# Recurrent mixer: where the convolution's taps stand in VectorE's order around the state scan

## The chip, the cores and the metric

The kernel runs on one core of one Trainium2 chip. The metric is the device time of one execution in microseconds (us). An engine here is TensorE (matrix products), VectorE and ScalarE (elementwise work), GpSimd or the queue that issues transfers. Each executes its own list of instructions in program order and waits on semaphores where the program says so.

## What is computed

Two stacks of transformer blocks over 512 tokens of width 1024, in 32 bits. The change concerns one of their twelve phases, the mixer of the first layer (`mixa` in the kernel). It is half recurrence, half convolution:

```python
def rwkv7_scan(r, w, k, v, kk, a):          # S_t = S_{t-1} diag(w_t) - (S_{t-1} kk_t)(kk_t*a_t)^T + v_t k_t^T
    def step(state, inp):
        r_t, w_t, k_t, v_t, kk_t, a_t = inp
        s_kk = jnp.einsum('bhvk,bhk->bhv', state, kk_t)
        state = (state * w_t[:, :, None, :] - s_kk[..., None] * (kk_t * a_t)[:, :, None, :]
                 + v_t[..., None] * k_t[:, :, None, :])
        return state, jnp.einsum('bhvk,bhk->bhv', state, r_t)
...
    y = rwkv7_scan(rh, hs(decay), kh, vh, kk, hs(a))        # 8 heads of 64
    y = group_norm(y) * lnx_g + lnx_b                       # written out in the reference
    y_a = (y + bonus) * g
    glu = c_val * jax.nn.sigmoid(c_gate)                    # 512 channels
    conv = lax.conv_general_dilated(glu, conv_w[:, None, :], ...) + conv_b   # 31 taps, causal, depthwise
    y_b = jax.nn.silu(layer_norm(conv, conv_ln_g, conv_ln_b, CONV_LN_EPS))
    return jnp.concatenate([y_a, y_b], axis=-1) @ w_out
```

The two halves are independent from the input projection to the concatenation.

## The kernel before

Every phase is a program for each engine: `pe` for TensorE, `act` for ScalarE, `dve` for VectorE, `pool` for GpSimd, `sp` for the queue that loads weights. The order within an engine is written out by hand; a planner has no part in it. Arrays lie with their features on the 128 partitions, in tiles of 128 features by 512 tokens.

The recurrence is computed in 16 chunks of 32 tokens. After the input projection (22 panels), products within the chunks give masked matrices (line 1711, `gram`); VectorE inverts triangular 32x32 matrices for all chunks and heads (lines 2107 and 2108); TensorE turns and multiplies the factors (lines 1718 to 1790) and makes the per-chunk transitions (line 1802, `outer`), which ScalarE copies out of PSUM. Then come token products in rounds (line 1826, `tokens`): after the fourth round VectorE adds their result to `rho` (line 2115), and TensorE goes on with eight more rounds, the first of which needs all four additions.

The scan proper is a loop over chunks c = 1 to 14. In each step TensorE multiplies the transition with the state (line 1844) and signals `fs_done`, and multiplies the state with `rho` for the output (line 1849). VectorE scales the state (line 2121), adds the outer product (line 2122), waits for `fs_done`, and adds the product in two halves to make the next state (line 2128), which signals `state_ready`, for which TensorE's next step waits.

After the scan ScalarE copies the output y (line 1943), TensorE sums it by heads (line 1854), VectorE centres it (line 2131), ScalarE squares it (line 1946), TensorE sums the squares (line 1691), and ScalarE takes four roots (line 1949, `head_roots` up to 5). VectorE makes the reciprocals (line 2134). TensorE spreads them over the partitions (line 1698, `head_spread`), and only behind that in its order come the column sums of the convolution's layer norm (line 1863), for which all 124 taps must be done (`conv_tap`). VectorE centres the convolution's result with them (line 2138), finishes the normed y (lines 2141 to 2143), and so on to the output projection, which begins at line 243.

The convolution is a list of 31 x 4 = 124 taps in VectorE's program. `conv(n)` issues the next n of them: the first four are a scaling with the bias (line 2065), the others multiply a shifted `glu` by a weight and add it to `acc` (line 2068). A tap needs nothing but the tap of four places before it and `glu`, which is complete long before. Nothing but the layer norm reads the result. In the kernel before, 44 taps stand ahead of the additions to `rho`, one in each of the 14 steps of the scan, and the other 66 behind the centring of y, ahead of the reciprocals.

Of the kernel before, what the change touches and what calls it, by code (L numbers as in the profile page):

```python
# [1612 lines left out]
def make_mixa(env):  # L1613
# [33 lines left out]
    def state(c):  # L1647
        return E2[0][:, 0] if c == 1 else S2[0][:, c - 2] if c < 10 else S2[1][:, c - 10]
# [315 lines left out]
    def dve(dve, idx, n, b):  # L1964
# [84 lines left out]
        def masked(kind, banks, dst, m):  # L2049
            for par in range(2):  # L2050
                dve.wait_ge(S("mats_done"), 2 * kind + par + 1)
                tt(dst[:, 16 * par:16 * par + 16, :], PS[:, banks[par], :].rearrange("p (h s) -> p h s", h=16),
                   con(m).unsqueeze(1).to_broadcast([128, 16, C]), ALU.mult).then_inc(S("mats_masked"), 1)

        taps = [(j, f) for j in range(CONVW) for f in range(4)]
        done = [0]

        def conv(count):

            for _ in range(min(count, len(taps) - done[0])):  # L2060
                j, f = taps[done[0]]
                src, w = glu[:, f, j:j + T], vec("cw", 4 * j + f)
                if j == 0:
                    dve.wait_ge(S("glu_made"), 4)
                    i = ve.tensor_scalar(acc[:, f, :], src, w, vec("cb", f), ALU.mult, ALU.add)
                else:
                    dve.wait_ge(S("conv_tap"), done[0] - 3)
                    i = stt(out=acc[:, f, :], in0=src, scalar=w, in1=acc[:, f, :], op0=ALU.mult, op1=ALU.add)  # L2068
                i.then_inc(S("conv_tap"), 1)
                done[0] += 1  # L2070
# [38 lines left out]
        ve.transpose(Tt.rearrange("p h t -> p t h"), Tp).then_inc(S("inverse"), 1)  # L2109
        masked(2, (6, 7), Gt, "mupi")  # L2110
        masked(3, (1, 2), Qt, "mupin")
        conv(44)
        for f in range(4):
            dve.wait_ge(S("round_done"), 4)
            tt(rho[:, f, :], rho[:, f, :], PS[:, BB[f], :], ALU.add).then_inc(S("factors_made"), 1)
        dve.wait_ge(S("ef_copied"), 16)
        for c in range(1, NCH - 1):
            if c > 1:
                dve.wait_ge(S("state_ready"), 2 * (c - 1))
            d = steps[c % 2]  # L2120
            st.done(tt(d, state(c), ends[:, :, c:c + 1].to_broadcast([128, NHP, 64]), ALU.mult))
            st.done(tt(d, d, E2[c // 8][:, c % 8], ALU.add))
            conv(1)
            dve.wait_ge(S("fs_done"), c)
            for par in range(2):
                rows = slice(64 * par, 64 * par + 64)
                f_s = PS[rows, BA[2 * (c % 2) + par], 0:256].rearrange("p (h v) -> p h v", h=NHP)
                tt(state(c + 1)[rows], d[rows], f_s, ALU.add).then_inc(S("state_ready"), 1)
        for f in range(4):
            dve.wait_ge(S("gn_sums"), f + 1)  # L2130
            stt(out=y[:, f, :], in0=PS[:, BA[f], :], scalar=-1.0 / HD, in1=y[:, f, :], op0=ALU.mult, op1=ALU.add).then_inc(S("centred"), 1)
        conv(len(taps))
        dve.wait_ge(S("head_roots"), 5)
        ve.reciprocal(recips, sums).then_inc(S("head_recips"), 1)
        dve.wait_ge(S("conv_tap"), 4 * CONVW)
        dve.wait_ge(S("gn_sums"), 13)
        for f in range(4):
# [11 lines left out]
        env["parts_dve"](dve, b["mix"], DT, HI0)  # L2149

    return dict(sp=sp, pool=pool, pe=pe, act=act, dve=dve, hi0=HI0)


# [125 lines left out]
```

## Time and profile before

| | us |
|---|---|
| three runs | 3999.42, 4002.21, 4023.23 |
| median of them | 4002.21 |
| the profiled execution | 3997.31 |
| its span | 3995.5 |

| engine | busy, us | share of the span |
|---|---|---|
| TensorE, products | 3707.4 | 93% |
| VectorE | 1927.5 | 48% |
| ScalarE | 1505.7 | 38% |
| GpSimd | 13.5 | 0% |

How to read it: the span is from the first to the last instruction of the profiled execution, and 1.8 us lie around it. The shares are averages over twelve phases; the mixer's recurrence takes less than 250 us of the span. The granted clock is TensorE's, as a part of 2.4 GHz: 1.00 is that, 0.50 is 1.2 GHz. The idle time that the timeline shows before an instruction carries the name of the engine and line that released it.

### The profile page before, as it was taken

How to read it: one execution, taken by the hardware profiler on the slowest of the kernel's cores; microseconds unless marked ns; L12 is line 12 of the kernel's file. 1: busy time of each engine (PE TensorE's matmuls, PEld its weight loads, DVE VectorE, ACT ScalarE, POOL GpSimd, SP SyncE). 2: the span in 40 equal slices, each digit the busy share in tenths (PEclk: the TensorE clock that was granted, in tenths of full speed). 3: DMA queues.
4: the chain of work that ended last, by engine and by line, in shares of the span. 5: the costliest groups of instructions: out<-in, count | busy, mean ns of one | idle time of the engine just before them, and what ended most of it. 6: DMA issues, size and time to landing. Idle time of an engine off the chain costs nothing.

```text
span 3995.5 us, 56056 instructions
## 1 busy us (share of the span) xinstructions
PE 3707.4 (93%) x21784; PEld 3056.4 (76%) x21784; DVE 1927.5 (48%) x2830; ACT 1505.7 (38%) x2293; POOL 13.5 (0%) x33
## 2 busy tenths in 40 slices
PE   8999986499999999999999998889999989899998
PEld 6887765378887887996678887668788876687887
DVE  3443476744425443234444424545676344456763
ACT  3323421243323333335443234544444335454432
POOL 0000000000000000000000000000000000000000
PEclk9999986699999999999999999999999989999999
DMA  3323210023232233220022332002232320023333
GB/s 112 99 92 97 69 54 4 6 79 99 94 96 79 97 94 94 90 89 6 19 80 97 93 94 87 1 17 90 85 100 92 96 86 1 27 81 94 96 95 94
DMA packets 84246, 297.16 MB, mean 74 GB/s; under 512 B 9520, under 2 KB 9520, under 8 KB 83696
## 3 DMA queue, kind: packets, MB, share of 16 engines
q1 hardware_dynamic: 82512, 288.24, 23.0%
q0 software_dynamic: 1568, 6.56, 0.5%
q8 instruction: 122, 2.00, 0.2%
q14 instruction: 44, 0.36, 0.0%
HBM read 292.66 MB, written 2.10 MB: 74 GB/s over the span
## 4 chain that ended last, share of the span: by engine, by line
PE 88%; DVE 6%; ACT 3%; issue 2%; DMA 1%; SPq 0%; DVEq 0%; ACTq 0%
PE PS L252 21%; PE PS L243 21%; PE PS L244 20%; PE PS L834 4%; PE PS L857 3%; PE PS L329 2%; PE PS L332 2%; PE PS L330 2%; PE PS L363 2%; PE PS L846 2%; DVE WK L2068 1%; PE PS L922 1%; PE PS L836 1%; PE PS L275 1%; ACT WHI L215 1%
## 5 line engine op out<-in xcount | busy, mean ns | idle before, releaser
L243 PE MATMUL PS<-WK_R,WHI 128*128 128x512 f32 (+1 forms) x3712 | 1443.8, 390 | 14.0 <-ACT WK_R L581 11.0
L244 PE MATMUL PS<-WK_R,WLO 128*128 128x512 f32 (+1 forms) x3712 | 1438.6, 388 | 0.0
L219 DVE TENSOR_TENSOR WLO<-RAW,WHI 128x1024 fp32r<-128x1024 f32 x563 | 689.2, 1225 | 1266.9 <-ACT WHI L215 1263.6
L215 ACT ACTIVATE WHI<-RAW 128x1024 fp32r<-128x1024 f32 x563 | 596.9, 1060 | 1038.8 <-PE PS L252 838.4
L243 PEld LDWEIGHTS PS<-WK_R,WHI 128*128 128x128 f32 x3712 | 699.5, 188 | 168.8 <-issue 20.2
L244 PEld LDWEIGHTS PS<-WK_R,WLO 128*128 128x128 f32 x3712 | 699.4, 188 | 141.7 <-issue 0.7
L252 PE MATMUL PS<-H_LO,WHI 128*128 128x512 f32 x2712 | 683.1, 391 | 4.5 <-DVE H_LO L436 4.2
L252 PEld LDWEIGHTS PS<-H_LO,WHI 128*128 128x128 f32 x2712 | 508.3, 188 | 119.8 <-DVE H_LO L436 16.3
L252 PE MATMUL PS<-HID_LO,WHI 128*128 128x512 f32 x1056 | 263.2, 389 | 0.0
L252 PEld LDWEIGHTS PS<-HID_LO,WHI 128*128 128x128 f32 x1056 | 198.0, 188 | 40.9
L329 PE MATMUL PS<-WHI,WK_R 128*128 128x256 f32 (+1 forms) x736 | 190.4, 291 | 5.0 <-DVE WLO L219 4.9
L330 PE MATMUL PS<-WLO,WK_R 128*128 128x256 f32 (+1 forms) x736 | 189.9, 290 | 0.0
L1004 DVE SCALAR_TENSOR_TENSOR SC<-SC,VEC 128x511 f32<-128x511 f32 x176 | 132.2, 751 | 111.5 <-ACT SC L971 99.6
L834 PE MATMUL PS<-WK 64*128 64x512 f32 (+5 forms) x384 | 178.3, 549 | 5.8 <-ACT WK L1121 3.4
L609 ACT ACTIVATE WK_R<-HID (+1 forms) x88 | 55.7, 633 | 261.0 <-DVE HID L626 261.0
L329 PEld LDWEIGHTS PS<-WHI,WK_R 128*128 128x128 f32 x736 | 140.4, 191 | 5.8 <-DVE WLO L219 3.8
L897 DVE TENSOR_REDUCE AS<-PS 128x1 f32<-128x512 f32 (+2 forms) x192 | 111.1, 580 | 65.3 <-PE PS L834 62.8
L971 ACT ACTIVATE SC<-SC,VEC 128x512 f32<-128x512 f32 x88 | 72.0, 818 | 182.3 <-DVE SC L994 182.3
L330 PEld LDWEIGHTS PS<-WLO,WK_R 128*128 128x128 f32 x736 | 140.5, 191 | 0.0
L606 ACT ACTIVATE SC<-SC 128x512 f32<-128x512 f32 x88 | 55.7, 632 | 159.4 <-DVE SC L620 159.0
L628 DVE TENSOR_TENSOR HID_LO<-HID,WK_R (+1 forms) x88 | 61.0, 693 | 86.8 <-ACT WK_R L609 86.8
L363 PEld LDWEIGHTS PS<-CON,SC 128*128 128x128 f32 x640 | 87.0, 202 | 18.0 <-ACT SC L511 6.7
(325 smaller groups left out, 3538.0 us busy)
## 6 DMA issues: line engine op xcount, KB each, us to landing
RAW<-in_ffn_gu SPq DMA_DIRECT2D x176, 512.0 KB, 3.4
RAW<-in_f_up SPq DMA_DIRECT2D x88, 512.0 KB, 3.7
RAW<-in_ffn_dn SPq DMA_DIRECT2D x64, 512.0 KB, 3.6
RAW<-in_c_in SPq DMA_DIRECT2D x32, 512.0 KB, 3.5
RAW<-in_f_dn SPq DMA_DIRECT2D x32, 512.0 KB, 3.5
RAW<-in_ffn_dn SPq DMA_DIRECT2D x32, 384.0 KB, 3.1
RAW<-in_a_in SPq DMA_DIRECT2D x22, 512.0 KB, 3.4
RAW<-in_b_out SPq DMA_DIRECT2D x16, 512.0 KB, 3.5
```

Source lines behind the costliest of these rows:

```text
L215: nc.scalar.activation(WHI[:, slot, :], RAW[:, slot, :], ACT.Copy).then_inc(S("w_hi"), 1)
L219: nc.vector.tensor_tensor(WLO[:, slot, :], RAW[:, slot, :], WHI[:, slot, :].bitcast(F32), ALU.subtract).then_inc(S("w_lo"), 1)
L243: pe.matmul(o, WHI[:, slot, w], hi(k), start=(first and b_ == 0), stop=False)
L244: pe.matmul(o, WLO[:, slot, w], hi(k), start=False, stop=False)
L252: mm = pe.matmul(o, WHI[:, p.nslot(s_), w], lo(k), start=False, stop=(last and b_ == len(ks) - 1))
L329: pe.matmul(o, hi(k, t), WHI[:, slot, w], start=(first and b_ == 0), stop=False)
L330: pe.matmul(o, hi(k, t), WLO[:, slot, w], start=False, stop=False)
L363: mm = pe.matmul(PS[:, b_, 128 * t:128 * t + 128], SC[:, k, 128 * t:128 * t + 128], ones, start=(first and t == 0), stop=(last and t == TT ...
L834: mm = pe.matmul(o, spec["q"](h, t), spec["k"](h, n), start=True, stop=extra is None)
L857: mm = pe.matmul(PS[:, 5 + U % 2, 0:spec["dv"]], spec["PT"](U % 3)[:, 128 * b:128 * b + 128], v, start=(b == 0), stop=(b == nb - 1))
L897: nc.vector.reduce_max(stat(1, U), PS[:, U % 3, 0:n], AX.X, negate=True).then_inc(S("at_max"), 1)
L1004: nc.vector.scalar_tensor_tensor(out=o, in0=s, scalar=vec("fcw", (idx * 3 + tap) * 2 * FT + part * FT + e), in1=o, op0=ALU.mult, op1=ALU.a ...
```

## The change

The 124 taps are issued in other blocks. 24 more stand ahead of the additions to `rho` (68 instead of 44). A new block of 34 stands between these additions and the first step of the scan. The tap in each of the 14 steps is gone. Behind the centring of y there are 6, then the reciprocals, and then the last 16. No instruction, wait or transfer is added or removed, and the programs of the other engines are the same.

```diff
@@ -2109,10 +2109,11 @@
         ve.transpose(Tt.rearrange("p h t -> p t h"), Tp).then_inc(S("inverse"), 1)
         masked(2, (6, 7), Gt, "mupi")
         masked(3, (1, 2), Qt, "mupin")
-        conv(44)
+        conv(68)
         for f in range(4):
             dve.wait_ge(S("round_done"), 4)
             tt(rho[:, f, :], rho[:, f, :], PS[:, BB[f], :], ALU.add).then_inc(S("factors_made"), 1)
+        conv(34)
         dve.wait_ge(S("ef_copied"), 16)
         for c in range(1, NCH - 1):
             if c > 1:
@@ -2120,7 +2121,6 @@
             d = steps[c % 2]
             st.done(tt(d, state(c), ends[:, :, c:c + 1].to_broadcast([128, NHP, 64]), ALU.mult))
             st.done(tt(d, d, E2[c // 8][:, c % 8], ALU.add))
-            conv(1)
             dve.wait_ge(S("fs_done"), c)
             for par in range(2):
                 rows = slice(64 * par, 64 * par + 64)
@@ -2129,9 +2129,10 @@
         for f in range(4):
             dve.wait_ge(S("gn_sums"), f + 1)
             stt(out=y[:, f, :], in0=PS[:, BA[f], :], scalar=-1.0 / HD, in1=y[:, f, :], op0=ALU.mult, op1=ALU.add).then_inc(S("centred"), 1)
-        conv(len(taps))
+        conv(6)
         dve.wait_ge(S("head_roots"), 5)
         ve.reciprocal(recips, sums).then_inc(S("head_recips"), 1)
+        conv(len(taps))
         dve.wait_ge(S("conv_tap"), 4 * CONVW)
         dve.wait_ge(S("gn_sums"), 13)
         for f in range(4):
```

## Rows read from the trace of the kernel before

**Rows 1.** The page, busy time: engine, us (share of the span), instructions.
```profile
PE 3707.4 (93%) x21784; PEld 3056.4 (76%) x21784; DVE 1927.5 (48%) x2830; ACT 1505.7 (38%) x2293; POOL 13.5 (0%) x33
```

**Rows 2.** Chain of waits, 560 to 790 us: start us, us, what.
```profile
671.69 0.75 DVE WK L2068
...
712.29 43.72 DVE WK L2068 x66
756.01 0.27 DVE ST L2134
756.33 5.74 PE PS L1698 x64
762.07 3.65 PE PS L1863 x8
...
783.56 0.77 PE PS L243
```

**Rows 3.** Timeline of VectorE: start us, us, operation, [idle before, releaser].
```profile
602.66 1.90 DVE L2065 TENSOR_SCALAR WK<-WK,VEC 128x512 f32<-128x512 f32 x4
604.48 26.57 DVE L2068 SCALAR_TENSOR_TENSOR WK<-WK,VEC 128x512 f32<-128x512 f32 x40
651.00 2.48 DVE L2115 TENSOR_TENSOR HID<-HID,PS 128x512 f32<-128x512 f32 x4 [19.94 <-PE PS L1826]
653.39 0.42 DVE L2121 TENSOR_TENSOR RS<-H,ST 128x256 f32<-128x256 f32 x1
...
669.87 0.87 DVE L2128 TENSOR_TENSOR WK<-RS,PS 64x256 f32<-64x256 f32 x2 [14.81 <-PE PS L1844]
670.77 0.43 DVE L2121 TENSOR_TENSOR RS<-WK,ST 128x256 f32<-128x256 f32 x1
...
672.47 0.87 DVE L2128 TENSOR_TENSOR WK<-RS,PS 64x256 f32<-64x256 f32 x2
...
703.76 0.87 DVE L2128 TENSOR_TENSOR HID<-RS,PS 64x256 f32<-64x256 f32 x2
...
765.82 2.48 DVE L2138 SCALAR_TENSOR_TENSOR WK<-PS,WK 128x512 f32<-128x512 f32 x4 [9.54 <-PE PS L1863]
```

**Rows 4.** Timeline of TensorE in the scan and behind it, the same columns.
```profile
668.70 1.12 PE L1844 MATMUL PS<-H,WK 64*64 64x64 f32 x16
...
670.79 1.12 PE L1844 MATMUL PS<-WK 64*64 64x64 f32 x16 [0.17 <-DVE WK L2128]
671.70 1.01 PE L1849 MATMUL PS<-HID,WK 64*64 64x32 f32 x16
673.40 1.12 PE L1844 MATMUL PS<-WK 64*64 64x64 f32 x16 [0.69 <-DVE WK L2128]
...
706.45 5.11 PE L1854 MATMUL PS<-WK,CON 128*128 128x512 f32 x8 [0.70 <-ACT WK L1943]
711.40 3.73 PE L1691 MATMUL PS<-CON,SC 128*128 128x128 f32 x32
```

**Rows 5.** Timeline of ScalarE, the same columns: copies from PSUM, last head root.
```profile
606.60 2.06 ACT L1934 ACTIVATE WK<-PS 128x512 f32<-128x512 f32 x4 [7.69 <-PE PS L1775]
...
632.40 2.06 ACT L1940 ACTIVATE H<-PS 128x512 f32<-128x512 f32 x4 [5.12 <-PE PS L1802]
...
715.17 0.27 ACT L1949 ACTIVATE ST<-PS,eps 128x8 f32<-128x8 f32 x1 [0.32 <-PE PS L1691]
```

**Rows 6.** Stretches: us, busy us by engine, granted clock (third from last).
```profile
669.87:704.63 34.76, 25.71 (x431) 23.82 (x428) 32.56 (x67) 0.00 (x0) 0.00 (x0) 0.50 0.01 2
705.00:710.00 5.00, 4.30 (x19) 2.25 (x18) 0.81 (x2) 2.70 (x5) 0.00 (x0) 0.57 0.00 0
715.00:720.00 5.00, 0.13 (x2) 0.00 (x0) 5.00 (x8) 0.27 (x1) 0.00 (x0) 0.96 0.00 0
755.00:760.00 5.00, 3.67 (x34) 3.67 (x36) 1.28 (x3) 0.00 (x0) 0.00 (x0) 0.50 0.00 0
760.00:765.00 5.00, 5.00 (x41) 3.27 (x38) 0.00 (x0) 0.00 (x0) 0.00 (x0) 0.95 0.00 0
```

## The prediction, before the result was known

> **What bounds the kernel now.** I read the page first. TensorE is busy for 93% of the span [rows 1], so a change that touches only VectorE's order can matter only where TensorE stands still. The change edits the `dve` program of the recurrent mixer, so I read the chain of waits in the stretch where that program runs, about 600 to 784 us. What the reader is to see there: most of the span has TensorE in the chain, but this stretch does not. It has one piece of 43.72 us that is VectorE alone, 66 taps in a row of the convolution (line 2068), with a reciprocal, the spreading product of line 1698 and the column sums of line 1863 one after another behind it [rows 2]. In that time TensorE has nothing that it may do, because its next order (line 1698) waits for the reciprocal, which stands behind all 66 taps in VectorE's queue.
>
> Then I read VectorE's timeline, to find where it is idle [rows 3]. There are two holes ahead of the scan: 19.94 us before the four additions to `rho` (line 2115, which wait for TensorE's fourth round of token products), and 14.81 us before the first state update (line 2128, which waits for the first product of line 1844). Last I read TensorE's timeline in the scan and behind it [rows 4], ScalarE's for the square roots [rows 5], and the granted clock in short stretches [rows 6].
>
> **The change, part by part.** Nothing is added or removed: 124 taps before, 44 + 14 + 66, and 124 after, 68 + 34 + 6 + 16. A tap inside a block costs 26.57 / 40 = 0.664 us, and the 66 give the same, 43.72 / 66 = 0.662 [rows 2, 3].
>
> *24 more taps ahead of `rho`.* The 44 taps run from 602.66 to 604.48 + 26.57 = 631.05. The additions start at 651.00, when TensorE is there [rows 3]. 24 x 0.664 = 15.9 us brings the taps' end to 647.0. Cost: nothing, hidden by TensorE's products, with 4.0 us to spare. Without that cover it would be 15.9 us. The new neighbours are ScalarE's copies of 632 to 646 us; four copies beside taps at 606.60 took 2.06 us and four without taps at 632.40 took 2.06 [rows 5], so neither disturbs the other.
>
> *34 taps between `rho` and the scan.* This is the part that costs. The additions are issued by 653.39, where the scan's first instruction starts now [rows 3]. 34 x 0.664 = 22.6 us, so that instruction starts at 675.97. The two preparations of a step (lines 2121 and 2122) take 671.69 - 670.77 = 0.92 us from start to tap, so the first state update starts at 676.89 instead of 669.87: **7.0 us late**. Of the 22.6 us, the 14.81 us hole and the one tap that already sat in it hide the rest. Queued behind the taps is the whole scan; TensorE's second product waits for this update, and TensorE stands still for those 7 us. The Trainium skill's page "TensorE: Matmul & The Clock Gate" (architectural detail of the array) says that ScalarE and VectorE execute strictly in order, which speaks against this part; the trace agrees, since VectorE idled 14.81 us before line 2128 with 66 taps still queued. An engine that took work out of order would make this term 0 and the sum 7.0 us better.
>
> *No tap within the scan.* A step takes 2.60 to 2.61 us: first updates at 669.87 and 672.47, last one at 703.76, so 13 periods in 33.89 us, 2.607 each [rows 3]. Without the tap (0.78 us from its start at 671.69 to 672.47 [rows 2, 3]) VectorE's own part is 1.83 us. But the update also waits for TensorE. Its loop: product of line 1844 starts at 668.70 and the update at 669.87, which is 1.17 us; two updates take 0.87 us; TensorE starts 0.05 us after them (670.74 to 670.79). Together 2.09 us [rows 3, 4]. TensorE's own work of a step ends at 671.70 + 1.01, so 1.92 us after its start at 670.79, and fits. So the scan will be bound by the round trip, period 2.09 us, and VectorE will wait 0.26 us a step. Gain 13 x (2.607 - 2.09) = **6.7 us**. Bounds: 0 (the period stays) and 13 x (2.607 - 1.83) = 10.1 us (VectorE alone). I take 2.09, because both legs of it are rows of this loop.
>
> *The tail: 22 taps instead of 66, and the reciprocal 60 taps sooner.* From the first of the 66 taps to the use of the column sums: 765.82 - 712.29 = 53.53 us [rows 2, 3]. After: 6 taps 3.98 us, in which the last head root (715.17 + 0.27 = 715.44 [rows 5]) comes in before the taps' end at 716.3, so the reciprocal doesn't wait; reciprocal 0.35 (0.32 from the 66 taps' end at 756.01 to TensorE's start at 756.33 [rows 2], and a little for the next tap's start); 16 taps 10.62, and 0.1 for the last one's end and the signal; then the sums of line 1863. The spreading product of line 1698 (5.74 us) starts at the reciprocal and lies beside the 16 taps, with 4.9 us to spare; without that cover it would cost its 5.74.
>
> What do the sums cost? They took 3.65 us with the clock at its upper level (2.4 GHz), since line 1698 ran right before them [rows 2, 6]. In the new order there is an idle stretch of about 5 to 7 us between line 1698 and them. Rows: after TensorE's last work at 715.13 the clock had fallen by 719.6 (0.96 of full speed on average in 715 to 720), and from a cold start at 756.33 it came back at about 760.5, 4.2 us later (0.50, then 0.95) [rows 4, 6]. The same kind of product, line 1854, took 5.11 us when the clock rose 2.85 us into it (0.57 in 705 to 710) [rows 4, 6]. At 4.2 us into it the price is 4.2 + (3.65 - 2.1) = 5.75. I take 5.4, between these two; bounds 3.65 (never cold) and 7.3 (cold throughout). Sum: 3.98 + 0.35 + 10.62 + 0.1 + 5.4 = 20.45, gain 53.53 - 20.45 = **33.1 us**, bounds 31.2 and 34.8.
>
> What follows the first use of the sums (line 2138), 17.7 us up to the output product of line 243 at 783.56 [rows 2], doesn't change.
>
> **The sum** is 7.0 - 6.7 - 33.1 = -32.8 us. Against the profiled execution, whose own time is 3997.3 us (span 3995.5 and 1.8 around it), that is 3964.5; against the median of the runs shown, 4002.2, it is 3969.4. The two differ by 5 us of scatter; I take 3967 between them.
>
> **Rivals.**
>
> *A. The clock comes up in the scan.* The scan ran at 0.50, the lower level of 1.2 GHz, throughout, and TensorE stood still for 0.69 us in each step [rows 4, 6]. After, it stands still for only 0.17 us a step. If the clock then goes to 2.4 GHz, the product's share of the round trip shrinks, and VectorE's 1.83 us a step is the bound: gain 10.1 instead of 6.7, and line 1854, which follows, takes 3.65 instead of 5.11. The Trainium skill, same page, Part 1, has half speed as the default and activity as what releases it, so this rule could bring it here. Sum: 7.0 - 10.1 - 1.5 - 33.1 = -37.7, with a sum product that isn't cold (3.65) -39.4: 3960 to 3962. Against it: these are small products of 64x64, and no row here shows such ones alone lifting the clock.
>
> *B. The scan gives nothing.* The 1.17 us of the round trip is from a single step, in which TensorE came straight from other work. If a product that starts from standstill needs 0.5 us more, the period stays at 2.61. The row of 673.40 with 0.69 us of idleness before it [rows 4] can't exclude it, since the tap covered that time. Sum 7.0 - 33.1 = -26.1, so 3974.
>
> *C. Slower.* The taps stretch in their new places, beside TensorE's token products and ScalarE's copies. With x us more on each tap it costs 64x less the 4.0 of spare ahead of `rho` (the first four are of another form), 34x before the scan and 22x behind it, so 120x - 4.0. That equals the 32.8 us at x = 0.307, a tap of 0.97 us. At 1.0 it is 36.3 us and the time just over 4000; at 1.1 it is 48.3 and the time 4013. Against it: 40 taps already ran beside such products and such copies at 0.664.
>
> *D. The change doesn't do what it says*, because something else takes the tail's place: the head roots or line 1698 end later than the 16 taps. Both have rows, 0.9 and 4.9 us of spare, and if both are cold and late by 3 us the gain falls by 2: 3969. I count it with the forecast.
>
> **How the numbers follow.** Forecast with D: 0.72. A: 0.12. B: 0.12. C: 0.02; 0.02 for what I don't see. The bounds taken together are -39.4 from the lower time, 3958, and -24.2 (no gain in the scan, cold sums) from the median, 3978; with some scatter of the runs the range is 3956 to 3982. What a measurement of this kernel can tell from no change is about 1%, 40 us. The forecast lies at 0.8%, inside it; A ends at 0.94 to 0.99% and with the scatter of the runs is over the line in nearly half of its cases, which gives 0.05, and the scatter of the forecast gives the rest: faster 0.12, same 0.85, slower 0.03.
>
> **What the profile after would show.** Four additions at line 2115 still at 651 with 4 us idle before them. A block of 34 taps up to 676, TensorE idle for 7 us. State updates 2.09 us apart (1.83 is A, 2.61 is B), clock at 0.50. Line 1698 at 717 beside taps, line 1863 at about 727.5 for 5.4 us, and the output product of line 243 at about 751 instead of 783.56. What would make me wrong: taps longer than 0.7 us ahead of `rho`, a scan period off 2.09, or a wait between line 1863 and the 16th tap.

## The result and the profile after

The kernel after takes 3970.59 us in the median of 13 runs (3959.27 to 3993.22), the kernel before 4000.77 in the median of 13 (3986.0 to 4023.23). The ratio is 0.9931, with an interval of 0.9909 to 0.9953: 0.7% faster, 30.2 us by the medians. I had predicted 3967, within 1% of before, and a change of -32.8 us.

The profiled execution of the kernel after was one of its longest, 3993.2 us. Its span is 3991.4, only 4.1 under that of before, though the part that was edited is 30.6 us shorter. So the comparison has to be made by stages, and the rest of the span looked at apart. First the edited part. I cut it from the start of the additions to `rho` to the start of the output product of line 243. Some line numbers have moved by one: the kernel after's 2122, 2123 and 2139 are before's 2121, 2122 and 2138, and 2128 is the same in both.

VectorE's timeline of the kernel after (start us, us, operation, idle before and its releaser), to be read against [rows 3]:

```profile
603.82 42.49 DVE L2068 SCALAR_TENSOR_TENSOR WK<-WK,VEC 128x512 f32<-128x512 f32 x64
650.45 2.48 DVE L2115 TENSOR_TENSOR HID<-HID,PS 128x512 f32<-128x512 f32 x4 [4.14 <-PE PS L1826]
652.85 22.61 DVE L2068 SCALAR_TENSOR_TENSOR WK<-WK,VEC 128x512 f32<-128x512 f32 x34
675.38 0.42 DVE L2122 TENSOR_TENSOR RS<-H,ST 128x256 f32<-128x256 f32 x1
...
676.29 0.87 DVE L2128 TENSOR_TENSOR WK<-RS,PS 64x256 f32<-64x256 f32 x2
...
678.45 0.87 DVE L2128 TENSOR_TENSOR WK<-RS,PS 64x256 f32<-64x256 f32 x2 [0.37 <-PE PS L1844]
...
704.37 0.87 DVE L2128 TENSOR_TENSOR HID<-RS,PS 64x256 f32<-64x256 f32 x2 [0.37 <-PE PS L1844]
...
718.25 10.59 DVE L2068 SCALAR_TENSOR_TENSOR WK<-WK,VEC 128x512 f32<-128x512 f32 x16
734.64 2.48 DVE L2139 SCALAR_TENSOR_TENSOR WK<-PS,WK 128x512 f32<-128x512 f32 x4 [5.80 <-PE PS L1863]
```

What is to be seen: the hole of 19.94 us ahead of `rho` has shrunk to 4.14; the hole of 14.81 us ahead of the first update is gone, and that update comes 25.84 us behind the additions' start instead of 18.87; each later update has a new wait of 0.37 us for TensorE; and the sums' use comes 20.6 us behind the centring instead of 53.5.

TensorE's timeline of the kernel after, same columns, to be read against [rows 4] and the products in [rows 2]:

```profile
667.62 1.12 PE L1844 MATMUL PS<-H,WK 64*64 64x64 f32 x16
...
677.21 1.12 PE L1844 MATMUL PS<-WK 64*64 64x64 f32 x16 [7.67 <-DVE WK L2128]
...
679.37 1.12 PE L1844 MATMUL PS<-WK 64*64 64x64 f32 x16 [0.24 <-DVE WK L2128]
...
707.06 6.30 PE L1854 MATMUL PS<-WK,CON 128*128 128x512 f32 x8 [0.70 <-ACT WK L1943]
713.20 3.73 PE L1691 MATMUL PS<-CON,SC 128*128 128x128 f32 x32
718.38 3.71 PE L1698 MATMUL PS<-CON,ST 128*64 128x128 f32 x64 [1.45 <-DVE ST L2134]
728.89 5.63 PE L1863 MATMUL PS<-WK,CON 128*128 128x512 f32 x8 [6.79 <-DVE WK L2068]
```

TensorE stands still for 7.67 us in front of the second step, the spreading product of line 1698 has moved beside the 16 taps, and 6.79 us of standstill now lie between it and the sums of line 1863.

The edited part by stages, in us, all worked out from starts in such timelines ("centred" is the end of the fourth instruction of line 2131):

| kernel | additions to first update | first to last update | to centred | to the sums' use | to line 243 | together |
|---|---|---|---|---|---|---|
| before | 18.87 | 33.89 | 8.53 | 53.53 | 17.74 | 132.56 |
| as predicted | 25.9 | 27.2 | 8.5 | 20.45 | 17.7 | 99.8 |
| after | 25.84 | 28.08 | 9.72 | 20.55 | 17.73 | 101.92 |
| after, second profile | 25.84 | 28.07 | 9.24 | 20.31 | 17.73 | 101.19 |
| after, third profile | 25.83 | 28.08 | 9.20 | 20.28 | 17.74 | 101.13 |

Now the rest of the span. The missing 26 us are in another phase, the attention of the second layer, three phases later. The stretches of the first profile of the kernel after (us, busy us of TensorE and of the others, and third from last the granted clock):

```profile
1790.00:1800.00 10.00, 10.00 (x25) 5.48 (x23) 3.15 (x10) 2.95 (x9) 0.00 (x0) 0.50 0.01 2
1850.00:1860.00 10.00, 10.00 (x28) 6.33 (x27) 2.29 (x8) 2.00 (x6) 0.00 (x0) 0.50 0.00 1
1870.00:1880.00 10.00, 10.00 (x50) 6.43 (x49) 4.49 (x16) 3.97 (x13) 0.00 (x0) 1.00 0.01 2
```

and one of the same phase in its second profile (execution of 3955.75 us):

```profile
1790.00:1800.00 10.00, 10.00 (x53) 6.63 (x52) 5.21 (x20) 4.90 (x17) 0.00 (x0) 1.00 0.00 0
```

In the first, TensorE is busy all the time from 1790 on, and yet the clock stays at 0.50 (1.2 GHz) for some 75 us; in 10 us it gets 25 products done instead of 53. From the first product of line 834 in this phase to the last it takes 175.0 us, and 139.9 in the second profile. The ten other profiles of this study, of all kernels, lie at 139.9 (eight) and 143.0 (two, each with 6.8 us at 0.50). So 35.1 us are lost here, and the other phases give some 9 back. The two profiles of one and the same kernel are 37.4 us apart in span, and 0.7 us of that is in the edited part. The kernel after thus doesn't have this stretch each time; whether the edit makes it likelier is taken up at the end of the experiments.

### The profile page after: what moved, and what is told of

Same layout as the page of the kernel before. It is cut to its first block, busy times and chain, and to the rows that moved or that the text cites. A ratio compares the mean times of both kernels' runs of the same rounds, so it can differ in the third digit from the quotient of the medians.

```text
span 3991.4 us, 56056 instructions
## 1 busy us (share of the span) xinstructions
PE 3736.0 (94%) x21784; PEld 3070.7 (77%) x21784; DVE 1926.5 (48%) x2830; ACT 1503.2 (38%) x2293; POOL 13.5 (0%) x33
## 4 chain that ended last, share of the span: by engine, by line
PE 88%; DVE 6%; ACT 3%; issue 2%; DMA 1%; SPq 0%; DVEq 0%; ACTq 0%
PE PS L252 21%; PE PS L243 20%; PE PS L244 20%; PE PS L834 4%; PE PS L857 3%; PE PS L329 2%; PE PS L332 2%; PE PS L330 2%; PE PS L846 2%; PE PS L363 2%; PE PS L836 1%; PE PS L922 1%; DVE WK L2068 1%; ACT WHI L215 1%; PE PS L275 1%
## 5 line engine op out<-in xcount | busy, mean ns | idle before, releaser
L252 PEld LDWEIGHTS PS<-HID_LO,WHI 128*128 128x128 f32 x1056 | 198.0, 188 | 40.9
L834 PE MATMUL PS<-WK 64*128 64x512 f32 (+5 forms) x384 | 188.8, 578 | 5.8 <-ACT WK L1121 3.4
```

The costliest lines, as they stand in the source:

```text
L252: mm = pe.matmul(o, WHI[:, p.nslot(s_), w], lo(k), start=False, stop=(last and b_ == len(ks) - 1))
L834: mm = pe.matmul(o, spec["q"](h, t), spec["k"](h, n), start=True, stop=extra is None)
```

## The experiments

The first four take one part of the change away or do one part alone, the fifth asks what bounds the new step, and all five are judged by the stage from the additions to line 243.

**Only the hole ahead of `rho`** (on the kernel before):

```diff
-        conv(44)
+        conv(68)
```

> Edit on the kernel before: 68 taps instead of 44 ahead of the additions to rho, everything else as before, so the block behind the centring of y shrinks from 66 to 42 taps. Measure: time from the start of the additions (line 2115) to the output product (line 243), 132.6 us before and 101.9 after. My theory (24 taps are hidden in the 19.9 us hole, the tail loses them one for one): additions still 4 us idle before them, scan unchanged at 2.61 us a step, stage 132.6 - 24 x 0.663 = 116.7 us. Rival (the taps stretch beside ScalarE's copies, or the tail is held by something else): additions late, or a stage above 120.

Measured: 116.43 us, by stages 18.61 + 33.89 + 8.94 + 37.26 + 17.73. The gain of 16.1 us is the 24 taps (15.9), as expected. One thing was not: VectorE did not idle ahead of the additions here. Its and TensorE's timelines of this kernel:

```profile
603.82 42.49 DVE L2068 SCALAR_TENSOR_TENSOR WK<-WK,VEC 128x512 f32<-128x512 f32 x64
646.22 2.48 DVE L2115 TENSOR_TENSOR HID<-HID,PS 128x512 f32<-128x512 f32 x4
```

```profile
645.04 0.31 PE L1826 MATMUL PS<-HID,SC 32*64 32x32 f32 x1 [0.69 <-issue]
648.81 2.39 PE L1826 MATMUL PS<-HID,WK 32*64 32x32 f32 x126 [3.45 <-DVE HID L2115]
```

TensorE's fourth round ended at 645.35, 0.87 us before the taps, and TensorE waited 3.45 us for the additions instead of the 2.62 of the kernels where the taps were done in time. The round's end moves: measured from the start of the transposition of line 2102 to the start of that last product, it was 72.6 us here and 77.6 in the kernel after, with up to 79.4 in its third profile. The standstills between are marked "issue", and they fall differently in each execution. In the seven profiles with 68 taps ahead of `rho` VectorE's spare goes from -0.9 (here) to 5.9 us (the kernel after, third profile), with a mean of 2.5. So the predicted 4.0 us of spare are one draw, and not the average.

**No block ahead of the scan** (on the kernel after; its 34 taps go behind the reciprocals):

```diff
-        conv(34)
```

> Edit on the kernel after: the block of 34 taps between rho and the scan is taken out, they go behind the reciprocals (50 instead of 16). My theory: the block costs 7.5 us in front of the scan and saves 34 x 0.663 = 22.5 behind it, so without it the first state update comes 7.5 us earlier, the tail is 22.5 longer, stage 101.9 + 15.0 = 116.9 us; the sums of line 1863 start cold all the same and take 5 to 6 us. Rival (the block costs more than its delay of the first update, for example because TensorE starts the scan from standstill and each step is slower for it): the period of the scan falls under 2.16 us without the block.

Measured: 117.15 us. Its first step, TensorE's rows and VectorE's (line 2127 is the update here):

```profile
666.30 0.32 PE L1826 MATMUL PS<-HID,WK 32*64 32x32 f32 x2 [1.23 <-issue]
666.54 1.12 PE L1844 MATMUL PS<-H,WK 64*64 64x64 f32 x16
```

```profile
667.78 0.87 DVE L2127 TENSOR_TENSOR WK<-RS,PS 64x256 f32<-64x256 f32 x2 [15.40 <-PE PS L1844]
669.94 0.87 DVE L2127 TENSOR_TENSOR WK<-RS,PS 64x256 f32<-64x256 f32 x2 [0.37 <-PE PS L1844]
```

The first update comes 18.67 us behind the additions' start, 7.2 sooner; the scan takes 28.06 us, 2.158 a step, the same as with the block; the tail is 43.49 instead of 20.55. So the block costs 7.2 and saves 22.9, and TensorE's standstill of 7.67 us ahead of the second step slows no later step. That rival falls. The rows show one thing more, which the account below needs: TensorE comes to this first product straight from line 1826, and the update still starts 1.24 us after it (667.78 - 666.54).

**A tap in each step again** (on the kernel after, tail unchanged):

```diff
-        conv(34)
+        conv(20)
...
+            conv(1)
             dve.wait_ge(S("fs_done"), c)
```

> Edit on the kernel after: one tap in each of the 14 steps again, taken from the block ahead of the scan (20 instead of 34); tail as after. My theory, with the measured period of 2.16 us: the first update is at its early place again, 7.5 us sooner, and 13 steps are 2.607 instead of 2.16, 5.8 us more; stage 101.9 - 7.5 + 5.8 = 100.2 us, so putting no tap within the scan is worth nothing by itself, or costs 1.7 us. Rival, as the step of the prediction had it (period 2.09, first update 7.0 late): 101.9 - 0.3 = 101.6 or more. A second rival: the scan's own gain is real and the block's delay is not, then it is 107.7.

Measured: 100.05 us, 18.33 + 33.85 + 9.63 + 20.51 + 17.73. VectorE's timeline:

```profile
650.33 13.34 DVE L2068 SCALAR_TENSOR_TENSOR WK<-WK,VEC 128x512 f32<-128x512 f32 x20
666.26 0.87 DVE L2129 TENSOR_TENSOR WK<-RS,PS 64x256 f32<-64x256 f32 x2 [1.02 <-PE PS L1844]
668.87 0.87 DVE L2129 TENSOR_TENSOR WK<-RS,PS 64x256 f32<-64x256 f32 x2
...
700.11 0.87 DVE L2129 TENSOR_TENSOR HID<-RS,PS 64x256 f32<-64x256 f32 x2
```

20 taps fit into the hole and leave 1.02 us of it; the steps are 2.60 us again. The first update is 7.5 us sooner than in the kernel after and the scan 5.8 us longer. So the part of the change that its name speaks of, no tap within the scan, gains nothing: by this trace it loses 1.1 to 1.9 us against the same kernel with 14 taps there (100.05 against 101.1 to 101.9). Both rivals, 101.6 or more and 107.7, lie above what was measured. A tap in a step costs 0.45 us of time, because 0.33 of its 0.78 fills the wait for TensorE; a tap too many ahead of the scan costs its whole 0.66.

**Only the reciprocals ahead** (on the kernel before):

```diff
-        conv(len(taps))
+        conv(6)
         dve.wait_ge(S("head_roots"), 5)
         ve.reciprocal(recips, sums).then_inc(S("head_recips"), 1)
+        conv(len(taps))
```

> Edit on the kernel before: only the reciprocals are moved, 6 taps ahead of them and 60 behind. My theory: line 1698 (5.74 us) is hidden beside the 60 taps, about 6.0 us with the signals, but TensorE then stands still for some 36 us, and the sums of line 1863 start cold: 5.6 instead of 3.65 us. Stage 132.6 - 6.0 + 1.9 = 128.5 us. Rival without the clock: 126.6. Rival in which the order of the reciprocals is free of effect: 132.6.

Measured: 129.55 us, 1.0 more than expected. TensorE's timeline of this kernel:

```profile
717.19 3.71 PE L1698 MATMUL PS<-CON,ST 128*64 128x128 f32 x64 [1.45 <-DVE ST L2134]
756.85 6.31 PE L1863 MATMUL PS<-WK,CON 128*128 128x512 f32 x8 [35.94 <-DVE WK L2068]
```

The tail alone went from 53.53 to 50.37. The spreading product is hidden, 6 us, but the sums behind 35.94 us of standstill take 6.31 us, where they took 3.65 in [rows 2]. Nearly half of what was hidden is paid back. In line 1854 this execution lost another 1.0 us against before (6.09 against 5.11), and its first update came 0.8 us sooner (18.05 against 18.87), so the stage is 3.0 us shorter. The rival without the clock (126.6) falls, and so does the one without any effect.

**Half a tap in each step** (on the kernel after; a tap over 512 tokens is issued as two over 256, seven taps taken from the last block):

```diff
+            conv(0.5)      # the next half: acc[:, f, cols], cols = 0:256 or 256:512
             dve.wait_ge(S("fs_done"), c)
```

> Edit on the kernel after: half a tap (256 of the 512 tokens) in each of the 14 steps of the scan, ahead of the wait for TensorE's product; the 7 taps come from the last block (9 instead of 16). VectorE waits 0.37 us in each step; half a tap takes about 256/512 x 0.55 + 0.11 = 0.39 us. My theory (the step is bound by the round trip with TensorE, not by VectorE): the period stays at 2.16 to 2.20 us and the tail is 7 x 0.663 = 4.6 us shorter, stage 101.9 - 4.6 + 0.3 = 97.6 us. Rival (VectorE's own work and the signals set the period): 2.16 + 0.39 = 2.55 us a step and stage 101.9 - 4.6 + 5.1 = 102.4.

Measured: 98.18 us, and a period of 2.336 us, between the two. The timeline of VectorE within a step:

```profile
681.27 0.42 DVE L2129 TENSOR_TENSOR RS<-WK,ST 128x256 f32<-128x256 f32 x1
...
681.73 0.42 DVE L2130 TENSOR_TENSOR RS<-RS,H 128x256 f32<-128x256 f32 x1
...
682.19 0.48 DVE L2071 SCALAR_TENSOR_TENSOR WK<-WK,VEC 128x256 f32<-128x256 f32 x1
...
682.70 0.87 DVE L2136 TENSOR_TENSOR WK<-RS,PS 64x256 f32<-64x256 f32 x2
```

The half tap takes 0.51 us up to the update, not 0.39: I had priced it like a tap within a block, and ahead of the update it costs about 0.12 more (a whole tap is 0.664 in a block and 0.78 in a step, [rows 2, 3]). That an instruction of another kind follows is not enough for this: in the kernel after the block of 34 ends at 652.85 + 22.61 = 675.46, and line 2122 starts at 675.38, before its end, while the update starts 0.03 us behind the end of its tap. What delays the update is not shown. With 1.83 of VectorE's own work that makes 2.34, so here VectorE is the bound again. But of the 0.51 us only 0.18 show in the period; 0.33 were hidden. That settles what bounds the kernel after's step: the round trip with TensorE at 2.16, not VectorE. In the tail only 9 taps stand behind the reciprocals, the sums start 2.2 us after line 1698 and take 3.70 us, so the seven taps bring 6.6 us (13.98 instead of 20.55), 4.6 by themselves and 1.9 by the sums, which find the clock still up.

**Taps in all holes.** The readings above say where VectorE is idle anyway, and a version was made from them (on the kernel after): 6 taps behind panel 19 of the projection, 3 between the halves of the second mask, 74 ahead of `rho`, 22 ahead of the scan, none in it, 6 ahead of the centring of y, 4 ahead of the reciprocals and 9 behind them.

```diff
+            if i == 19:
+                dve.wait_ge(S("factors_made"), 24)
+                conv(6)
...
-        masked(1, (0, 4), Nt, "mup")
+        masked(1, (0, 4), Nt, "mup", 3)      # three taps between its halves
...
-        conv(68)
+        conv(74)
...
-        conv(34)
+        conv(22)
...
+        conv(6)
         for f in range(4):
             dve.wait_ge(S("gn_sums"), f + 1)
...
-        conv(6)
+        conv(4)
```

> Edit on the kernel after: the taps are laid into all idle places of VectorE: 6 behind panel 19 of the projection (4.0 us idle), 3 between the halves of line 2052's second mask (2.4 us idle), 74 ahead of rho (4.1 us more to fill), 22 instead of 34 ahead of the scan, none in it, 6 while ScalarE and TensorE make the sums for the centring (3.9 us idle), then 4 ahead of the reciprocals and 9 behind them. My theory: first update 7.5 us earlier; behind the centring 0.7 and 7 x 0.663 = 4.6 us less; TensorE stands still for only 2 us between lines 1698 and 1863, so that it is still at 2.4 GHz and takes 3.65 instead of 5.6. Together 7.5 + 0.7 + 4.6 + 2.0 = 14.8 us: stage 87.1 us, time about 3956. Rival (the holes in the projection are paid for by TensorE, which waits for VectorE there): part of it comes back ahead of line 2115. Rival (the clock falls all the same): 89.

Measured: 3951.38 us in the median, against 3998.46 for the kernel before on the same chip; the ratio is 0.9882 (0.9867 to 0.9896). It is faster than the kernel before, and by the medians than the kernel after in both series that have the two (3963.68 and 3966.19, below, with some overlap of single runs). The stage is 86.98 us: 18.40 + 28.08 + 9.49 + 13.28 + 17.73. TensorE's timeline, and the stretch of line 1863:

```profile
711.81 3.71 PE L1698 MATMUL PS<-CON,ST 128*64 128x128 f32 x64 [0.74 <-DVE ST L2140]
717.68 3.70 PE L1863 MATMUL PS<-WK,CON 128*128 128x512 f32 x8 [2.16 <-DVE WK L2070]
```

```profile
717.68:721.38 3.70, 3.70 (x8) 1.44 (x8) 0.00 (x0) 0.00 (x0) 0.00 (x0) 1.00 0.00 0
```

The clock does not fall in 2.16 us of standstill, as it had in 6.79. A part of the rival is there too: 74 taps end at 652.3, and TensorE had been done with its fourth round 1.1 us before. The taps behind panel 19 and in the mask lie ahead of that. From the first instruction of line 2085 (2087 in this version) in this mixer to the transposition of line 2102 (2107) it is 157.8 us here and 156.4 in the second profile, against 157.3 before and 156.4 to 157.0 in the three profiles of the kernel after. So some 0.5 to 1 us may have come back in the projection in one profile, and nothing in the other. From the transposition to line 243 it is 165.5 us, against 179.9 in the first profile of the kernel after and 210.4 before.

**The kernel after again**, with the version above in the same series:

> The kernel after itself, on the same chip as the version above and in another five rounds, for a comparison of the two and for a second profile. My theory: stage 101 to 103 us, with the scan at 2.16 us a step; the rest of the scatter of the runs (3959 to 3993) comes from the granted clock in later phases: in the first profile it was at 0.50 from about 1790 to 1870 us where the kernel before had 0.92 to 1.00. If that is chance, a second profile mostly lacks it and is 20 to 30 us shorter. If the change brings it, it is there again.

Measured: 3963.68 us in the median (3955.75 to 3997.45), ratio 0.9931 (0.9905 to 0.9958). The stage is 101.19, and the stretch of attention at 0.50 is absent from this profile, shown above. A third series of both:

> The kernel after, another series, beside the kernel before on the same chip. In the two series so far 4 of 19 runs of it lay 28 to 38 us above the others (3992 to 3997 against 3956 to 3978), and 1 of 24 runs of the kernel before did (4023); the one whose trace I have had the granted clock at 0.50 for some 75 us of the attention phase behind the mixer, with TensorE busy. Theory 1 (chance: the clock of that phase falls in some executions of any of these kernels): both kernels show it, about 1 run in 8, and the rest of the runs of after lie at 3956 to 3978. Theory 2 (the change brings it, by the time at which that phase starts): after again has 1 or 2 of 6 and before none. In both, the middle of the runs is 30 to 35 us under that of before.

> The version with taps in all idle places, another series in the same rounds. Both theories: 3948 to 3957, 12 us under the kernel after and some 47 under before, stage from line 2115's additions to the output product 87 us. Theory 1 lets a run at 3980 to 3990 appear here too, theory 2 does not say.

Measured: the kernel after 3966.19 us in the median, ratio 0.990 (0.9878 to 0.9923), 40.9 under before where 30 to 35 were expected, and none of its six runs above 3971. The version with all holes filled 3957.9, ratio 0.989 (0.9863 to 0.9917), 8.3 under the kernel after instead of 12, with one run at 3977.55; the stage 101.13 and 87.79. The kernel before had two runs at 4015 and 4023 in this series. So of 25 runs of the kernel after, four lie 28 to 33 us above the median of the others, and single runs of the other two kernels lie 16 to 22 us above theirs. Neither theory came true as it was written: the change doesn't bring the long runs each time (1 of 6, then 0 of 6), but none of the 46 runs of the other two kernels lies as far above its median. That 4 of 25 against 0 of 46 is chance is possible and not shown, and whether the start time of the attention phase makes the long runs likelier stays open.

## Why the prediction was right, point by point

- *24 more taps ahead of `rho` are free, 4.0 us to spare.* Right in the profile of after (4.14). What I took for a fixed spare changes from execution to execution, and once was negative.
- *34 taps make the first update 7.0 us late.* 25.84 - 18.87 = 6.97. Every number of this term came from rows of the same instructions. That it fits to 0.1 us is partly luck: where the first update waits for TensorE's rounds (no block, or one of 20 or 22 taps) it came 18.05 to 18.87 us behind the additions' start in seven profiles, and before has the largest of these; with the block it is 25.83 or 25.84 in three. So the block's price is 7.0 to 7.8 us, 7.2 in the experiment without it.
- *No tap within the scan gains 6.7 us, period 2.09.* It gained 33.89 - 28.08 = 5.8, period 2.160. The mechanism was right, the round trip with TensorE is the bound, which the half tap shows. The term was mis-sized at the 1.17 us from TensorE's start to the update. I had it from one step of the kernel before. In the kernel after it is 678.45 - 677.21 = 1.24, and thirteen times 0.07 is the 0.9 us missing. Rival B would have put this down to TensorE's start from a standstill, with 0.5 us for it. It isn't that: in the kernel without the block TensorE comes to its first step from line 1826, and it is 1.24 all the same. What goes with the difference is the tap that the edit removes. In the four kernels with a tap between the step's two preparations and the update, the first step has 1.17; in the versions without one, the steps that wait for TensorE have 1.23 or 1.24. Why a tap there saves 0.07 us is not shown.
- *The tail gains 33.1 us.* 53.53 - 20.55 = 33.0. Within it, the sums of line 1863 took 5.63 us, where I had put 5.4 between rows of the fast and of the slow clock (5.39 and 5.37 in the other two profiles). The reciprocals did not wait, and line 1698 took 3.71 us instead of the 5.74 I had laid beside the 16 taps, so that 6.79 us of standstill followed it.
- *Between the last update and the centring nothing changes.* This I had not even written as a term, and it lost 1.2 us (0.7 in the other two profiles): line 1854 took 6.30 us instead of 5.11. The row of before was a lucky one. In the profiles of this study the same eight products took 5.11 to 6.62 us, according to where in them the clock rose.
- *Behind the sums nothing changes.* 17.73 against 17.74.
- *Rival A, the clock rises in the denser scan.* It did not:

```profile
676.29:705.24 28.95, 24.94 (x416) 23.20 (x416) 22.79 (x54) 0.00 (x0) 0.00 (x0) 0.50 0.01 2
```

That is the scan of the kernel after, TensorE at 1.2 GHz throughout with 0.24 us of standstill a step. *Rival C* needed taps of 0.97 us; they took 42.49 / 64 = 0.664 and 22.61 / 34 = 0.665.

The sum of the stages is 7.0 - 5.8 + 1.2 - 33.0 = -30.6 us, against -32.8 predicted and -30.2 by the medians. That the last two agree so well is luck: by the medians of the second and third series it is -34.8 and -40.9, though the edited part took the same there to 0.8 us. The whole gain is in the tail. The block ahead of the scan and the empty scan take 7.0 and give 5.8 up to the last update. The block pays even so, since its 34 taps are missing from the tail (22.9 us). Better left out was the move of the last 14 of them from the steps into the block, as the experiment with the taps back in the scan shows.

## What to carry to other kernels

Filler work belongs where its engine waits anyway, and its price is what is left over: here 0 in a hole, 0.45 of 0.78 us in a step that waits 0.33, and all of 0.66 in a block with nothing beside it. Behind a chain of dependent products, put the small instruction that releases the other engine ahead of the filler, but leave the other engine no long standstill before its next product, since that one then starts at the slow clock. And judge such an edit by the stages of its trace: the three profiles of the kernel after agree there to 0.8 us, while two of them are 37 us apart in span.

## What the runs showed of the hardware

- TensorE's clock stayed at 0.50 for some 75 us in a phase in which it was busy without a gap, in one execution, and was at 1.00 in the same phase of another. It cost 35.1 us of the 37.4 between them.
- Eight products of 128x512, after work at 2.4 GHz and 2.2 us of standstill, took 3.70 us, behind 6.8 us 5.4 to 5.6, behind 29 to 36 us 6.0 to 6.3.
- From the start of TensorE's 16 products of 64x64 to the start of the VectorE instruction that waits for them it was 1.17 us where a tap stood ahead of that instruction (four kernels), and 1.23 to 1.24 where none did, both after other products and from a standstill.
- A tap of 128x512 on VectorE cost 0.664 us in a block and 0.78 ahead of the state update. Behind a block, line 2122, of another kind, started 0.08 us before the block's end; the update started 0.03 us behind the end of its tap.
